# Expert weights of a mixture-of-experts layer: one 3 MB transfer per slot, in place of three of 1 MB

## What is computed

```python
def moe(x, router_w, router_b, w_gate, w_up, w_down, s_gate, s_up, s_down):
    scores = jax.nn.sigmoid(xt @ router_w)
    _, idx = lax.top_k(scores + router_b, TOP_K)          # 8 of 64
    gate = jnp.take_along_axis(scores, idx, axis=1)
    gate = gate / gate.sum(-1, keepdims=True) * ROUTE_SCALE
    ...
    def expert_rows(args):                                # for each block of rows of one expert
        h = jax.nn.silu(xb @ w_gate[e]) * (xb @ w_up[e])
        return (h @ w_down[e]) * g[:, None]
```

## Time and profile before

| | us |
|---|---|
| median of 3 runs | 2177.84 |
| lowest and highest of them | 2176.98, 2180.71 |
| the profiled execution | 2181.59 |
| its span, first to last instruction | 2179.8 |
| PE busy in it | 2027.2 (93%) |
| VectorE, ScalarE, GpSimd busy | 737.0, 402.0, 262.3 |

### The profile page before, as it was taken

The page is one execution under the profiler, slowest core; times in us unless marked ns, Lnnn a source line. Parts: engine busy times, 40 slices in busy tenths (PEclk is TensorE's granted clock), DMA queues, the critical chain, the costliest instruction groups (busy, mean ns, idle before and its releaser), DMA issues. The chain is left out here.

```text
span 2179.8 us, 26889 instructions
## 1 busy us (share of the span) xinstructions
PE 2027.2 (93%) x8690; PEld 1011.0 (46%) x8690; DVE 737.0 (34%) x1991; ACT 402.0 (18%) x881; POOL 262.3 (12%) x253
## 2 busy tenths in 40 slices
PE   8999898999999999977999888899999999999976
PEld 4553454444444444433448455554444444444432
DVE  4662252222222222225110777544222222222216
ACT  2102121111111111110001556311111111111110
POOL 0000301111111111100210000300111111111110
PEclk9999999999999999998998899999999999999998
DMA  7132235999999999969100100215799999999957
GB/s 224 9 61 97 102 141 222 394 410 409 402 402 389 406 392 402 386 247 334 16 0 35 44 1 2 83 58 233 311 397 399 413 404 400 400 410 405 395 226 326
DMA packets 126146, 566.09 MB, mean 260 GB/s; under 512 B 40705, under 2 KB 41473, under 8 KB 71169
## 3 DMA queue, kind: packets, MB, share of 16 engines
q1 hardware_dynamic: 97856, 498.06, 58.1%
q0 software_dynamic: 28224, 67.16, 7.9%
HBM read 539.84 MB, written 59.77 MB: 275 GB/s over the span
## 5 line engine op out<-in xcount | busy, mean ns | idle before, releaser
L439 PE MATMUL moe_bank<-moe_weights,moe_xgT 128*128 128x512 f32 x1024 | 455.4, 598 | 22.8 <-DMA moe_weights<-in_ex_w_up 22.4
L439 PEld LDWEIGHTS moe_bank<-moe_weights,moe_xgT 128*128 128x128 f32 x1024 | 189.4, 190 | 238.9 <-issue 214.8
L747 DVE TENSOR_TENSOR moe_hid<-moe_sil,moe_bank 128x256 f32<-128x256 f32 x98 | 41.3, 421 | 672.5 <-ACT moe_sil L622 672.5
L472 PE MATMUL moe_bank<-moe_weights,moe_hidT 128*128 128x512 f32 x512 | 230.5, 593 | 0.0
L442 PE MATMUL moe_bank<-moe_weights,moe_xgT 128*64 128x512 f32 x512 | 226.6, 595 | 0.0
L442 PE MATMUL moe_bank<-wide,moe_xgT 128*64 128x512 f32 x512 | 226.6, 595 | 0.0
L315 POOL DMA_INDIRECT y<-moe_xy,moe_rows x98 | 98.6, 1006 | 951.0 <-DVE moe_idx L727 586.9
L622 ACT ACTIVATE moe_sil<-moe_bank 128x256 f32<-128x256 f32 x98 | 37.6, 383 | 664.0 <-PE moe_bank L439 462.6
L755 DVE TENSOR_SCALAR moe_xy<-moe_bank,moe_sgate 128x512 f32<-128x512 f32 x98 | 73.6, 751 | 219.5 <-PE moe_bank L472 142.0
L472 PEld LDWEIGHTS moe_bank<-moe_weights,moe_hidT 128*128 128x128 f32 x512 | 92.4, 191 | 93.4 <-issue 93.4
L300 POOL DMA_INDIRECT moe_xy<-h,moe_idx x98 | 99.8, 1018 | 265.0 <-DVE moe_idx L727 237.4
(11 more groups left out here) (348 smaller groups left out, 2423.7 us busy)
## 6 DMA issues: line engine op xcount, KB each, us to landing
moe_weights<-in_ex_w_gate SPq DMA_DIRECT2D x96, 1024.0 KB
moe_weights<-in_ex_w_up SPq DMA_DIRECT2D x96, 1024.0 KB
moe_weights<-in_ex_w_down SPq DMA_DIRECT2D x96, 1024.0 KB, 20.9
wide<-in_ex_w_gate SPq DMA_DIRECT2D x34, 1024.0 KB
wide<-in_ex_w_up SPq DMA_DIRECT2D x34, 1024.0 KB
wide<-in_ex_w_down SPq DMA_DIRECT2D x34, 1024.0 KB
moe_weights<-y SPq DMA_DIRECT2D x18, 1024.0 KB, 21.3
wide<-y SPq DMA_DIRECT2D x8, 1024.0 KB, 8.0
```

The costliest lines, as they stand in the source:

```text
L439: mm = pe.matmul(bG[:, :], xgT[:, n, :], wgu[j][:, :, n, :], start=(n == 0), stop=(n == KC - 1))
L472: mm = pe.matmul(bY[half][:, :], hidT[:, n, :], wdn[j][:, n, cols], start=(n == 0), stop=(n == HC - 1))
```

## The change

The weights of an expert are laid out anew in memory ahead of the launch: for each partition its parts of gate, up and down side by side, 24 KB without a gap. A slot is loaded by one transfer of 3 MB with one semaphore. It is asked for when the down product of its step is done, for all three parts. Slots 2 and 3 are asked for one behind the other. PE waits for the whole slot ahead of gate/up and doesn't wait for weights ahead of down.

```diff
-        def load_gu(sp, e, j):
-            for k, src in enumerate((w["ex_w_gate"], w["ex_w_up"])):
-                sp.dma_start(wgu[j][:, k], src[layer, ds(e, 1)].rearrange("o (p c) f -> p (o c) f", c=KC)).then_inc(gu_landed[j], 16)
-
-        def load_dn(sp, e, j):
-            sp.dma_start(wdn[j][:, :, :], w["ex_w_down"][layer, ds(e, 1)].rearrange("o (p c) n -> p (o c) n", c=HC)).then_inc(dn_landed[j], 16)
+        def load_slot(sp, e, j):
+            sp.dma_start(spaces[j], w["ex_weights"][layer, ds(e, 1)].rearrange("o p n -> p (o n)")).then_inc(slot_landed[j], 16)
...
             for n, j in ((0, 3), (1, 0), (2, 1)):
                 e = sp.value_load(owner_id[0:1, n:n + 1], min_val=0, max_val=E - 1)
-                load_gu(sp, e, j)
-                load_dn(sp, e, j)
+                load_slot(sp, e, j)
             e = sp.value_load(owner_id[0:1, 3:4], min_val=0, max_val=E - 1)
             sp.wait_ge(sh_gu_done, NT)
-            load_gu(sp, e, 2)
             sp.wait_ge(sh_dn_done, NT)
-            load_dn(sp, e, 2)
+            load_slot(sp, e, 2)
             e = sp.value_load(owner_id[0:1, 4:5], min_val=0, max_val=E - 1)
             sp.wait_ge(gu_done, 1)
-            load_gu(sp, e, 3)
             sp.wait_ge(dn_done, 1)
-            load_dn(sp, e, 3)
+            load_slot(sp, e, 3)
...
-                gate_up_free(0)
-                load_gu(sp, owner_of(0), 0)
-                gate_up_free(1)
-                load_gu(sp, owner_of(1), 1)
-                down_free(0)
-                load_dn(sp, owner_of(0), 0)
-                gate_up_free(2)
-                load_gu(sp, owner_of(2), 2)
-                load_gu(sp, owner_of(3), 3)
-                down_free(1)
-                load_dn(sp, owner_of(1), 1)
-                down_free(2)
-                load_dn(sp, owner_of(2), 2)
-                load_dn(sp, owner_of(3), 3)
+                for k, js in ((0, (0,)), (1, (1,)), (2, (2, 3))):
+                    sp.wait_ge(dn_done, b + k + 1)
+                    sp.sem_inc(loading, 1)
+                    for j in js:
+                        e = sp.value_load(owner_id[0:1, ds(SLOTS * (t + 1) + j + 1, 1)], min_val=0, max_val=E - 1)
+                        load_slot(sp, e, j)
...
                 if not paired(t, k):
                     j = 3 if k == STEPS - 1 else k
-                    pe.wait_ge(gu_landed[j], 32 * uses(t, k) + 32)
+                    pe.wait_ge(slot_landed[j], 16 * uses(t, k) + 16)
                 else:
-                    pe.wait_ge(gu_landed[2], 32 * t + 32)
-                    pe.wait_ge(gu_landed[3], 32 * uses(t, k) + 32)
+                    pe.wait_ge(slot_landed[2], 16 * t + 16)
+                    pe.wait_ge(slot_landed[3], 16 * uses(t, k) + 16)
...
+def expert_layout(w):
+
+    layers, experts = w["ex_w_gate"].shape[:2]
+    parts = [w[k].reshape(layers, experts, P, -1) for k in ("ex_w_gate", "ex_w_up", "ex_w_down")]
+    return np.ascontiguousarray(np.concatenate(parts, axis=3))
```

## The result

| | before | after |
|---|---|---|
| median, us | 2179.28 | 2465.71 |
| lowest to highest, us | 2176.98 to 2181.67 | 2463.58 to 2469.64 |
| ratio, with its 95% interval | | 1.1315 (1.1298 to 1.1332) |
| span of the profiled execution, us | 2179.8 | 2464.9 |
| mean granted clock of PE | 0.976 | 0.927 |

A forecast was written before the change was run, and what follows sets the result against it. PE and DMA were taken as both full in the expert loops. Rounds of 35.5 + 9.3 + 1.9 + 0.9 = 47.6 us, 30 of them, add 337.7 us, plus 3.8 ahead of the loop: 2519 us, range 2400 to 2590.

The forecast's parts named there:

- the forecast case: The main case in the two expert loops: rounds of 45.5 to 49 us, 2456 to 2562 us in all, chance 0.60.
- Requests move later: Expert loops: gate and up parts, 8 of 12 MB a round, wait for down; 12.1 us remain until the paired gate/up.
- Landing 21.4 us after the down, stall 9.3 us: Paired gate/up: 0.84 + 17.2 + 2.4 + 1.0 us until slots 2 and 3 land, against 12.1 us.
- Clock, 1.9 us: PE behind each stall at the paired gate/up: granted clock about half for a while, 1.9 us lost a round.
- Slot 1, 0.9 us of stall: Slot 1's gate/up: 0.84 + 9.8 + 2.4 = 13.0 us to land against 12.1, 0.9 us a round.
- Slot 0 lands in time, fewer issues are worth nothing: Loop: slot 0 lands at about 31 us, wanted at 35; SP's 130 transfers in place of 390 gain nothing.
- Ahead of the loop +3.8 us: Before the loops, both layers: slot 3's first reload 0.9 us late, first gather 1 us later, each per layer.
- The slot 3 part: Slot 3's first reload in each layer now falls behind one down: 0.9 us of stall a layer.
- the 24 KB rows: Loop's weight transfers: 24 KB in place of 8 KB rows, bounds 0.3 us less and 390 GB/s flow, taken as nothing.
- Rival A: Paired gate/up: fewer, larger transfers lift the rate until DMA no longer bounds; rounds 35.51 us, 2153 us, chance 0.02.
- Rival B: Paired gate/up: same stall but cheaper, landing 19.8 us, slot 1 in time; rounds 43.2 to 44.9, centre 2410 us, chance 0.22.
- Rival C and D: Loop: more steps' gather and scatter wait, 2615 us, chance 0.11; or rows cut into small packets, 2582 us, chance 0.05.

## Why the prediction was right, and where its terms were off

The forecast said slower, by a stall at the paired gate/up in 30 rounds, with the half clock behind it, and in the range 2400 to 2590 us. That is what the trace shows. Its rounds of 45.6 us lie at the lower edge of the forecast case (45.5 to 49). Point by point:

- *Requests move later, the window is 12.1 us, only the pair's 6 MB overrun it*: right. The version with early requests has no stall at the pair, late requests in the old layout have it, and the pair alone makes it.
- *Landing 21.4 us after the down, stall 9.3 us*: PE starts after 20.1 us (19.8 for the landing, 0.3 behind it), and the stall is 8.0. Too long by 1.3 us a round, 39 us in all.
- *Clock, 1.9 us*: 2.1 us, by the round (45.6 - 35.5 - 8.0) and by the run with PE kept busy (64 us in all).
- *Slot 1, 0.9 us of stall*: none. 27 us too many. The sum also had it in the wrong place: slot 1's gate/up is the step that lies inside the pair's 12.1 us (L439 at 1686.85 in the earlier trace rows), so a wait there takes its length off the pair's wait and adds nothing to the round. The late requests in the old layout show this.
- *Round 47.6 us*: 45.7. The sum of the three.
- *Slot 0 lands in time, fewer issues are worth nothing*: no wait at either place, right.
- *Ahead of the loop +3.8 us*: the first gathers are waited for by 5.4 and 6.2 us, where it was 4.0 and 3.5, 4.1 us more. I had put 1 us for each layer within bounds of 0 and 5. The slot 3 part (0.9 us each) didn't come, for the reason that slot 1's didn't. The span rose by 285.1 us, the 30 rounds by 30 x 45.63 - 1090.3 = 278.6 us (45.63 is the mean of both layers, from the first L414 to the last); outside them are 6.5 us. These gathers are 4.1 of it. The last gate/up of each layer behind a stall is outside too: it takes 9.9 and 10.0 us in place of 7.0, 5.9 us more. So 3.5 us were gained elsewhere, which wasn't followed.

The term that failed is the one that was "taken as nothing": the 24 KB rows. I looked at them only for the rate of flow (bound -0.3 us) and for the gathers ahead of the loop. There I wrote that a gather might get its turn only after each 24 KB row, and didn't carry the same thought into the loop, where it would mean that the weights lose less to gather and scatter. I charged the pair 2.4 + 1.0 us for these and slot 1 2.4 us, prices from rounds with 8 KB packets. With 8 KB packets they come out: in the late requests in the old layout the pair landed 21.5 us after the down, against my 21.4, and slot 1 was late by 0.9 us. That this run also took 2519.2 us, where 2519 was the forecast, is in part luck. Its round is 47.5 us, of which 9.7 are stalls, the pair's 8.8 and slot 1's 0.9. I had 10.2 by counting slot 1's 0.9 us twice, and 1.9 us for a slow clock that took 2.2. The changed kernel is that run less 53 us for one transfer of 24 KB rows in place of three of 8 KB.

*Rival A* (larger transfers lift the rate, faster): no. The pair came 8 us past the window; larger rows gave 6 us in all where the requests stayed early. The Trainium skill's table of rates against transfer size ("DMA: Bandwidth & Descriptors", section on bandwidth: 341 GB/s at 1 MB, 425 at 16 MB, for transfers issued from GpSimd, where these come from SP) would have more: the measured gain, with 2 MB and 1 MB in place of three times 1 MB, is 0.27% of the kernel. *Rival B* (cheaper stall): half true. Its 19.8 us is where the landing came, and slot 1 was in time as it had it, though for smaller prices of gather and scatter and not for the rows; but it let the clock go. Its rounds ended at 44.9 us and the measured ones are 45.6. *Rival C and D*: no.

## What to carry to other kernels

When transfers are merged, ask first when the merged one may be asked for: it waits for the last reader of all its parts, and here 8 of 12 MB a round came to be asked for one step later. Hold the bytes that become due at one moment, over the rate of flow, against the time until the first reader; that sum gave 9.3 us of stall where 8.0 were measured. Then look which waits lie inside one another, since those don't add. A layout with longer rows can be had without the late request: keep one transfer for each reader.

## What the runs showed of the hardware that I had not expected

- How the transfers of one queue are cut goes with how another queue fares beside it. One transfer of 24 KB rows for a slot: median landing of scatters 13.6 us, and a slot of 3 MB in time; three of 8 KB rows: 9.2 us, and slot 1 0.9 us late. It was worth 53 us where the weights were on the critical path. That the size of the packets does it is likely, not shown.
- A stall costs more than its length on PE: 8.0 us of waiting were followed by 2.1 us lost at half clock. Idle matmuls in the waiting time gave those 64 us back. They have to be sized to end before the wait does: one float32 matmul of 512 columns was two instructions of 0.43 us, and 17 of them took 14.7 us and became the bound.
- Cutting the gathers from 128 to 16 rows made the changed kernel 13 us slower, not faster. This stays open.
